# The memory's key and value products at every second normalization tile, with two buffers for their raw weights

## The reference, cut to what matters

```
h = RMSNorm(x, g_norm)                      # 2048 + 128 rows, input of everything that follows
kv = RMSNorm(mem, g_mem) @ w_mem_kv         # (256 x 1024) @ (1024 x 1024)
mk, mv = kv[:, :512], kv[:, 512:]           # both are outputs; a later stage attends to them
```

## Time and profile before

| | |
|---|---|
| median of three runs | 3358.83 us (3356.28 to 3361.95) |
| the profiled execution | 3362.2 us |
| its span, first to last instruction | 3360.5 us |
| the normalization stage, to the first load of the next one | 112.9 us |
| PE busy over the span | 3019.1 us (90%) |
| granted TensorE clock, mean over the span | 0.95 |

### The profile page before, as it was taken

How to read it: one execution, slowest core, us unless ns; L and a number is a source line. 1 busy time by engine, 2 the same in 40 slices (tenths; PEclk the granted TensorE clock), 3 DMA queues, 4 the chain that set the end, 5 groups by cost and what they waited for, 6 DMA issues and landing times. The chain is left out here.

```text
span 3360.5 us, 50789 instructions
## 1 busy us (share of the span) xinstructions
PE 3019.1 (90%) x19627; PEld 2499.5 (74%) x19627; DVE 1417.4 (42%) x2011; ACT 989.5 (29%) x1827; POOL 872.7 (26%) x846
## 2 busy tenths in 40 slices
PE   5799999999999999986988988989968956999798
PEld 5688888888888888874766766766747734977687
DVE  4431111000000000007997997988956612533333
ACT  3551111111111111104454444444537823200121
POOL 4241121111111111102433433434425510433100
PEclk8899999999999999997998999999979966999899
DMA  4322222221222212218457456544546523744443
GB/s 170 110 74 73 94 87 72 70 76 65 73 70 71 73 68 73 69 47 226 159 161 208 155 166 206 164 148 158 165 128 185 169 67 91 222 159 155 168 136 113
DMA packets 308291, 415.55 MB, mean 124 GB/s; under 512 B 26577, under 2 KB 186961, under 8 KB 307697
## 3 DMA queue, kind: packets, MB, share of 16 engines
q1 hardware_dynamic: 276320, 310.76, 30.1%
q0 software_dynamic: 31760, 101.87, 8.3%
HBM read 309.93 MB, written 102.63 MB: 123 GB/s over the span
## 5 line engine op out<-in xcount | busy, mean ns | idle before, releaser
L385 PE MATMUL prj_bank<-hidden_hi,prj_w_hi 128*128 128x512 f32 (+2 forms) x2320 | 833.5, 359 | 9.9 <-DVE prj_w_lo L439 9.9
L387 PE MATMUL prj_bank<-hidden_hi,prj_w_lo 128*128 128x512 f32 (+2 forms) x2320 | 829.4, 357 | 0.0
L386 PE MATMUL prj_bank<-hidden_lo,prj_w_hi 128*128 128x512 f32 (+2 forms) x2320 | 829.1, 357 | 0.0
L385 PEld LDWEIGHTS prj_bank<-hidden_hi,prj_w_hi 128*128 128x128 f32 x2320 | 437.5, 189 | 64.5 <-DVE prj_w_lo L439 10.3
L429 ACT ACTIVATE prj_z<-prj_bank 128x512 f32<-128x512 f32 x290 | 155.0, 534 | 1112.5 <-PE prj_bank L387 1112.2
L387 PEld LDWEIGHTS prj_bank<-hidden_hi,prj_w_lo 128*128 128x128 f32 x2320 | 437.3, 188 | 55.1
L386 PEld LDWEIGHTS prj_bank<-hidden_lo,prj_w_hi 128*128 128x128 f32 x2320 | 437.6, 189 | 53.6
L437 DVE CAST prj_w_hi<-prj_w 128x1024 fp32r<-128x1024 f32 x58 | 40.2, 693 | 893.1 <-PE prj_bank L387 882.1
L901 POOL TENSOR_TENSOR stk_beta<-stk_beta,stk_left 128x1024 f32<-128x1024 f32 (+4 forms) x160 | 282.4, 1765 | 478.1 <-DVE stk_left L816 478.1
L486 POOL DMA_DIRECT2D scratch_zT<-prj_z x240 | 130.8, 545 | 981.7 <-ACT prj_z L429 964.9
L765 ACT ACTIVATE stk_beta<-stk_z 128x1024 f32<-128x1024 f32 (+2 forms) x224 | 181.8, 812 | 350.8 <-PE stk_z L952 272.6
(11 more groups left out here) (226 smaller groups left out, 4425.1 us busy)
## 6 DMA issues: line engine op xcount, KB each, us to landing
stk_kd<-in_cache_sb_k SPq DMA_DIRECT2D x64, 1024.0 KB, 7.1
stk_vd<-in_cache_sb_v SPq DMA_DIRECT2D x64, 1024.0 KB, 5.3
scratch_zT<-prj_z POOLq DMA_DIRECT2D x144, 256.0 KB, 2.3
prj_w<-in_w_in SPq DMA_DIRECT2D x58, 512.0 KB, 3.8
mrg_gate<-scratch_zT SPq DMA_DIRECT2D x24, 768.0 KB, 4.4
scratch_zT<-prj_z POOLq DMA_DIRECT2D x48, 192.0 KB, 2.1
mrg_u_raw<-scratch_uT SPq DMA_DIRECT2D x9, 1024.0 KB, 9.1
fin_a_raw<-scratch_mgT SPq DMA_DIRECT2D x17, 512.0 KB, 4.7
```

The source lines that it names most:

```text
L385: pe.matmul(out, w_hi[u][:, k, :], hi[:, k, first:first + width], start=k == 0, stop=False)
L386: pe.matmul(out, w_hi[u][:, k, :], lo[:, k, first:first + width], start=False, stop=False)
L387: last = pe.matmul(out, w_lo[u][:, k, :], hi[:, k, first:first + width], start=False, stop=k == KC - 1)
```

## The change

The product of chunk c moves from tile c + 3 to tile 3 + 2c, on PE's, ACT's and DVE's streams alike; its turned rows follow two tiles later, so the last chunk's are turned behind the last tile, at a step T = 19 that PE has now. The raw weights get two buffers, each with a semaphore of its own, and their load stands ahead of every second tile load. POOL's loop, the wait of `empty` for the stores, and the numbers of instructions, transfers and bytes stay as they are.

```diff
-    FIRST_PRODUCT, FIRST_ROWS = 3, 5
+    product_at = {3 + 2 * c: c for c in range(NMC)}
+    rows_at = {5 + 2 * c: c for c in range(NMC)}
...
-        w_raw, w_hi, w_lo = m.sb("w", [P, KC, P]), m.sb("w_hi", [P, KC, P], F32R), m.sb("w_lo", [P, KC, P], F32R)
+        w_raw = [m.sb(f"w{u}", [P, KC, P]) for u in (0, 1)]
+        w_hi, w_lo = m.sb("w_hi", [P, KC, P], F32R), m.sb("w_lo", [P, KC, P], F32R)
...
-        w_loaded, w_hi_done, w_lo_done = m.sem("w_loaded"), m.sem("w_hi_done"), m.sem("w_lo_done")
+        w_loaded = [m.sem(f"w_loaded{u}") for u in (0, 1)]
+        w_hi_done, w_lo_done = m.sem("w_hi_done"), m.sem("w_lo_done")
...
-            for T in range(4, len(tiles) + 4):
-                c = T - 4
-                if c < NMC:
-                    wait(sp, w_lo_done, c)
-                    sp.dma_start(w_raw[:, :, :], w_mem[:, :, c * P:c * P + P]).then_inc(w_loaded, 16)
+            for T in range(4, len(tiles) + 2):
+                c = T // 2 - 2
+                if T % 2 == 0 and c < NMC:
+                    wait(sp, w_lo_done, c - 1)
+                    sp.dma_start(w_raw[c % 2][:, :, :], w_mem[:, :, c * P:c * P + P]).then_inc(w_loaded[c % 2], 16)
                 if T < len(tiles):
                     load(T)
...
-                if 0 <= T - FIRST_PRODUCT - 1 < NMC:
-                    empty(T - FIRST_PRODUCT - 1)
+                if T - 1 in product_at:
+                    empty(product_at[T - 1])
...
-                if 0 <= T - FIRST_ROWS - 1 < NMC:
-                    copy_rows(T - FIRST_ROWS - 1)
+                if T - 1 in rows_at:
+                    copy_rows(rows_at[T - 1])
...
-            for T in range(len(tiles)):
-                turn(T)
-                if 0 <= T - FIRST_PRODUCT < NMC:
-                    products(T - FIRST_PRODUCT)
-                if 0 <= T - FIRST_ROWS < NMC:
-                    turn_rows(T - FIRST_ROWS)
+            for T in range(len(tiles) + 1):
+                if T <= LAST:
+                    turn(T)
+                if T in product_at:
+                    products(product_at[T])
+                if T in rows_at:
+                    turn_rows(rows_at[T])
...
             def split(c):
-                pool.wait_ge(w_loaded, 16 * c + 16)
+                pool.wait_ge(w_loaded[c % 2], 16 * (c // 2) + 16)
                 wait(pool, kv_summed, c)
```

More of the change, by code:

```diff
@@ L146, in place @@
             kind, t = tiles[T]
-            return (hid_m if kind == "m" else hid)[h][:, :, t * P:t * P + P]
+            if kind == "m":
+                return hid_m[h][:, :, t * P:t * P + P]
+            return hid[h][:, :, t * P:t * P + P]
         @block.sync
@@ L275, in split @@
             def split(c):
-                pool.wait_ge(w_loaded, 16 * c + 16)
+                pool.wait_ge(w_loaded[c % 2], 16 * (c // 2) + 16)
                 wait(pool, kv_summed, c)
-                pool.tensor_copy(w_hi[:, :, :], w_raw[:, :, :]).then_inc(w_hi_done, 1)
+                pool.tensor_copy(w_hi[:, :, :], w_raw[c % 2][:, :, :]).then_inc(w_hi_done, 1)
                 pool.wait_ge(w_hi_done, c + 1)
-                pool.tensor_tensor(w_lo[:, :, :], w_raw[:, :, :], f32(w_hi[:, :, :]), ALU.subtract).then_inc(w_lo_done, 1)
+                pool.tensor_tensor(w_lo[:, :, :], w_raw[c % 2][:, :, :], f32(w_hi[:, :, :]), ALU.subtract).then_inc(w_lo_done, 1)
             def store(c):
```

## The result

The changed kernel takes 3368.19 us (median of 11 runs, 3364.26 to 3373.74) against 3358.38 us before (median of 11, 3351.89 to 3363.80). The ratio is 1.0030, 95% interval 1.0020 to 1.0039: it is slower by 9.8 us. The forecast was 3370.8 us, a difference of 12.0.

What follows compares the result with a forecast made beforehand. No engine is full; a chain of waits between engines bounds the stage. 4 x 15.1 + 3 x 10.5 = 91.9 us plus a 6.6 us tail makes 98.5 against 86.5: 3358.8 + 12.0 = 3370.8 us, range 3363 to 3379.

Steps and rivals of the forecast that it cites:

- The chain and the lost overlap: Product, split, store, landing, square, scaling, transposes and next product now follow one another, without overlap: +12.0 us.
- the gate: ACT's `empty` waits for the store that left the same `kv` buffer two chunks before: four places, 30.3 us before.
- Split to store: On POOL, from a split's start to the issue of the `kv` store: 3.40 us.
- Store's issue to the empty: From the `kv` store's issue to the `empty` waiting for its landing: 2.5 us taken, ends 2.3 and 4.07.
- Empty to scaling: From `empty` through square, accumulator, root and reciprocal to the next tile's scaling: 1.98 us.
- scaling to transposes: From the start of a tile's scaling to its transposes on PE, without POOL's subtraction beside it: 1.33 us.
- Bursts in gated rounds: A tile's eight transposes and a product's 24 matmuls on PE, to the next split, starting at low clock: 5.9 us.
- Gated rounds: Split start to split start with a wait for the `kv` store: four of 15.1 us; three ungated of 10.5.
- The tail: After the last product: transposes, rounding, last rest, rows' copy, value store and its landing, 6.6 us.
- Full clock: Rival: PE runs all seven transposes-and-product pieces at 2.4 GHz, difference only +0.8 us, 3360 us; chance 0.12.
- Slow landing: Rival: stores land as slowly as before, +18.3 us, or PE at half clock throughout, +20.4; about 3378; chance 0.18.
- The gate that doesn't bind: Rival: store c - 2 is out before product c ends, all rounds 10.5 us, -6.4 us, 3352 us; chance 0.05.

Runs made afterwards that it cites:

- two ways to remove the gate: Changed kernel with kv store c - 2 issued ahead of the split of chunk c: 3351.28 us; changed kernel with three kv buffers: 3350.89 us.
- two ways to let the store land later: Changed kernel with one raw weight buffer again: 3377.04 us; changed kernel with the rows' store issued ahead of the kv store: 3372.52 us.
- the late empty: Changed kernel with ACT's `empty` one tile later, behind the next tile's square: 3345.22 us, ratio 0.9963.
- the early store: kv store c - 2 issued ahead of the split of chunk c: changed kernel 3351.28 us; kernel before 3354.26, with two raw buffers 3348.40.
- both edits: Changed kernel with the early store and the late empty together: 3338.48 us, ratio 0.9938.
- a fill: Changed kernel with 48 unread matmuls in PE's idle time ahead of the next tile, in each of four gated rounds: 3359.79 us, ratio 1.0004.

## Why the prediction was right, by its own steps

**The chain and the lost overlap.** Right, and shown from four sides: two ways to remove the gate give the same 105.4; two ways to let the store land later lengthen the stage; the late empty restores the overlap with the gate in place; and the early store is worth 2.9 us (7.6 with two raw buffers) where the overlap exists, against 20.2.

**The terms.** Split to store 3.40 us, as forecast. Store's issue to the empty: 2.27, 2.42, 2.12 and 2.10 us, mean 2.23, where 2.5 were taken; the choice of the uncontended value stores over the contended row was right, and by the contended one the forecast would have been 6.3 us higher. The transfer's row itself has a median of 2.0 us. For this the fit in the Trainium skill, "DMA: Bandwidth & Descriptors", section "Anatomy of one DMA", makes an estimate of 2.3 us; the trace agrees within 0.3. Empty to scaling 1.97 and scaling to transposes 1.34, against 1.98 and 1.33. Bursts in gated rounds took 6.3 us on average instead of 5.9, in the ungated 5.64, 5.64 and 5.51. PE stood for 7.9 to 8.2 us ahead of the first kind, and for 3.6 to 3.9 ahead of the second. The length of the wait does not settle it, as the shortest of the four gated bursts, 5.74 us, stands behind the longest wait, 8.18; where in a burst the clock rises stays open. Gated rounds took 15.26 instead of 15.1, ungated 10.24, 10.24 and 10.10 instead of 10.5. From the split of chunk 1 to the end of the last product, 117.21 - 25.59 = 91.6 us against 91.9. That it comes so close is luck in part, as errors of opposite sign cancelled there: 4 x 0.42 = 1.7 us too little on the gated bursts, against 4 x 0.27 = 1.1 too much on the landings and 0.9 too much on the three ungated rounds.

**The tail.** Forecast 6.6 us and 0.83 to the next stage's load, 7.4. Measured 125.61 - 117.21 = 8.4. This is the one term that was mis-sized beyond cancelling, by 1.0 us. The store goes out 4.0 us after the product, where 4.3 were forecast, but from its issue to the next load it takes 4.36 us and not 2.3 + 0.83. The landing is the expected 2.2; the remaining 2.1 us, where a last rest needed 0.83, are not resolved by the trace: the step that failed is to carry the 0.83 over from a stage that ended with a VectorE instruction to one that ends with a landing. In the runs with the early store and with both edits the same distance is 4.35.

**The stage and the whole.** The stage is 12.7 us longer, the forecast was 12.0; the medians differ by 9.8, with an interval of 6.7 to 13 that holds both. The profiled spans differ by 7.1 only, and most of the missing 5.6 lies in a stage that the change does not touch. The merge stage, from its first load to that of the final stage, took 320.7 us before and 315.9 after, in the same code; over the thirteen profiled executions of this study it lies between 312.6 and 320.7, though its code is the same in all of them. That is a scatter of 8 us, beside the 12 us between the fastest and the slowest of the eleven runs of the kernel before (3351.89 to 3363.80); why it varies stays open.

**Rivals.** Full clock: false without a fill. The fill shows that a burst can run so, in 4.10 us where the rival's sum had 4.3 and the gated bursts took 6.3. Slow landing: false in the changed kernel (2.23 us from issue to empty), true with one raw buffer (3.81). The gate that doesn't bind: false, and its 18.4 us of stage are what the early store brought (20.2).

## What to carry to other kernels

When work is moved to a later step in a hand-ordered schedule, ask for each engine in order which instruction the moved step now stands behind, and what ran in its wait before; here the gate cost 0.7 us a round (1.9 with two raw buffers) as long as the next product did not need the instruction behind it, and 5 us a round once it did. A second buffer for a load is worth what that load's wait costs on the chain, which is read from the gate that ends last and not from the sum of waits. The cheap remedies were orders, not memory: a store issued as soon as its data exist, and an emptying put behind the next tile's first instruction, together 33 us of stage.

## What the runs showed of the hardware

- A 128 KB store from POOL's queue landed in 2.0 to 2.2 us in quiet queues (the changed kernel, four stores) and in 3.2 to 4.0 us when a 512 KB load was issued 0.1 us behind it (the run with one raw buffer, four stores).
- Where VectorE's scaling and GpSimd's subtraction overlap, one of them is stretched, in these rows the one that starts later: the scaling took 2.67 us instead of 1.28 behind a running subtraction, the subtraction 3.23 instead of 2.33 behind a running scaling.
- Eight transposes and 24 matmuls took 5.7 to 6.9 us after 8 us of idleness, at granted clocks of 0.56 to 0.69. After a filled wait they took 4.1 us at 1.00 in three places and 5.5 us at 0.72 in one.
- Where a stage ended with a store, the next stage's first load came 2.1 us after its landing (the changed kernel); where it ended with a VectorE instruction, 0.83 us after that (the kernel before).
